# A fused attention and feed-forward step: weight loads behind the third unit's store, stack loads behind bias loads, sample copies behind splits, kept rows returned in three pieces

## The reference, cut to what matters

```
fq, fk, fv, ff, dq, dk, dv, iq, ik, iw = split(x @ w_in)         # 2892 columns, rotary on dq, dk, iq, ik
logf   = log_sigmoid(ff + b_forget)
fox    = causal attention, 8 heads x 64, logits + cumulative logf
score  = sum_h iw[h] * relu(iq[h] @ ik.T);  top 256 admissible keys per query
dsa    = attention of 8 heads (2 key heads) on these keys
h      = layer_norm(ALPHA * x + concat(fox, dsa) @ w_out)
f      = (silu(h @ w_gate) * (h @ w_up)) @ w_down                # D_FF = 2816
y      = layer_norm(ALPHA * h + f)
```

## Time and profile before

| | us |
|---|---|
| median of 3 runs | 1430.89 (1428.64 to 1433.03) |
| the profiled execution | 1433.38 |
| its span, first to last instruction | 1431.6 |
| TensorE busy | 1372.8 (96%) |
| VectorE busy | 986.7 (69%) |
| ScalarE busy | 695.2 (49%) |
| GpSimd busy | 531.6 (37%) |
| DMA moved | 192.27 MB, mean 134 GB/s |

### The profile page before, as it was taken

How to read it: one execution, slowest core, us unless ns; L and a number is a source line. 1 busy time by engine, 2 the same in 40 slices (tenths; PEclk the granted TensorE clock), 3 DMA queues, 4 the chain that set the end, 5 groups by cost and what they waited for, 6 DMA issues and landing times.

```text
span 1431.6 us, 23837 instructions
## 1 busy us (share of the span) xinstructions
PE 1372.8 (96%) x8985; PEld 1221.6 (85%) x8985; DVE 986.7 (69%) x1820; ACT 695.2 (49%) x1268; POOL 531.6 (37%) x571
## 2 busy tenths in 40 slices
PE   7989999999999899899999999999999998999997
PEld 7869989987777677687889999999999996778886
DVE  4489899778784989847775455555645656846488
ACT  5579889548684788710242223333223234524331
POOL 3632435622231022324465555555555551010011
PEclk9999999999999999999999999999999999999999
DMA  7102322358834211421124443454344449847554
GB/s 237 55 13 62 109 66 77 84 140 223 200 104 121 59 54 38 148 93 44 44 91 150 159 148 127 154 170 164 119 138 153 147 160 358 286 140 247 167 168 155
DMA packets 142738, 192.27 MB, mean 134 GB/s; under 512 B 21416, under 2 KB 99208, under 8 KB 142624
## 3 DMA queue, kind: packets, MB, share of 16 engines
q1 hardware_dynamic: 142624, 190.75, 42.2%
HBM read 134.59 MB, written 46.15 MB: 126 GB/s over the span
## 4 chain that ended last, share of the span: by engine, by line
PE 38%; POOL 8%; DVE 5%; issue 3%; ACT 1%; DMA 1%; POOLq 0%; DVEq 0%; SPq 0%; ACTq 0%
PE ffn L2676 21%; PE ffn L2191 6%; POOL w_lo L2957 5%; POOL gated L2966 3%; PE ffn L2776 3%; PE ffn L2777 3%; PE ffn L2778 3%; DVE down_lo L3041 2%; ACT w_hi L2832 1%; DMA down_raw<-in_w_down 1%; DVE rows L3175 1%; PE ffn L2650 1%; PE ffn L2795 0%; PE ffn L2793 0%; DVE ln_stats L2079 0%
## 5 line engine op out<-in xcount | busy, mean ns | idle before, releaser
L2957 POOL TENSOR_TENSOR w_lo<-w_S,w_hi 128x512 fp32r<-128x512 f32 x88 | 119.7, 1360 | 107.5 <-ACT w_hi L2832 107.5
L2676 PE MATMUL ffn<-h_T_hi,w_hi 128*128 128x264 f32 x704 | 145.6, 287 | 2.3 <-POOL w_lo L2957 2.1
L2676 PE MATMUL ffn<-h_T_lo,w_hi 128*128 128x264 f32 x704 | 143.7, 285 | 0.0
L2932 ACT CAST down_hi<-down_raw 128x1024 fp32r<-128x1024 f32 (+1 forms) x77 | 89.5, 1173 | 109.9 <-DMA down_raw<-down_w 46.5
L2676 PE MATMUL ffn<-h_T_hi,w_lo 128*128 128x264 f32 x704 | 142.8, 283 | 0.0
L2095 POOL TENSOR_TENSOR ln_rstd<-ln_var_eps,ln_power 128x1 f32<-128x1 f32 (+1 forms) x18 | 29.4, 1632 | 277.1 <-DVE ln_var_eps L2075 144.8
L3041 DVE TENSOR_TENSOR down_lo<-down_raw,down_hi 128x1024 fp32r<-128x1024 f32 (+1 forms) x77 | 105.0, 1387 | 35.0 <-ACT down_hi L2932 34.7
L2776 PE MATMUL ffn<-down_hi 128*128 128x512 f32 x308 | 121.4, 394 | 6.1 <-DVE down_lo L3041 6.1
L2832 ACT CAST w_hi<-w_S 128x512 fp32r<-128x512 f32 x88 | 54.7, 621 | 143.3 <-PE ffn L2676 141.9
L2777 PE MATMUL ffn<-down_lo,down_hi 128*128 128x512 f32 x308 | 121.0, 393 | 0.0
L2778 PE MATMUL ffn<-down_hi,down_lo 128*128 128x512 f32 x308 | 121.0, 393 | 0.0
(11 more groups left out here) (416 smaller groups left out, 3948.3 us busy)
## 6 DMA issues: line engine op xcount, KB each, us to landing
down_raw<-down_a SPq DMA_DIRECT2D x77, 256.0 KB, 3.5
gate_raw<-in_w_gate SPq DMA_DIRECT2D x11, 1024.0 KB, 6.7
up_raw<-in_w_up SPq DMA_DIRECT2D x11, 1024.0 KB, 6.4
down_t<-in_w_down SPq DMA_DIRECT2D x44, 256.0 KB, 4.1
down_w<-down_t SPq DMA_DIRECT2D x22, 512.0 KB, 3.4
down_raw<-in_w_down SPq DMA_DIRECT2D x22, 512.0 KB, 5.7
down_raw<-down_w SPq DMA_DIRECT2D x44, 256.0 KB, 4.0
down_a<-down_s SPq DMA_DIRECT2D x10, 1024.0 KB, 4.1
```

What stands on the lines that cost most here:

```text
L2676: mm = nc.tensor.matmul(pp[:, bank[to] + ch, 0:PIECE], l, x[name][:, k, ch * PIECE:(ch + 1) * PIECE], start=opens and k == 0 and i == 0, s ...
L2932: nc.scalar.copy(hs[:, 0:n], raws[s % RAWS][:, 0:n]).then_inc(hi_done, 1)
L2957: nc.gpsimd.tensor_tensor(w_lo[n % 2][:, :, :], weight(m, SCHEME[q][0]), f32(w_hi[n % 2][:, :, :]), ALU.subtract).then_inc(w_lo_done, 1)
```

## The change

- Projection: for groups 2 to 7, load_w(g + 2) goes from the beginning of group g to between the third and the fourth unit's stores.
- Attention: stack_head(6) goes from batch 6 to batch 7, behind load_bias(5); stack_head(7) from batch 7 to batch 9, behind load_bias(6).
- Start of the feed-forward: the low parts of ("S", "rest") go behind those of T3, tiles 2 and 3; the second sum then comes before them and S4 after.
- Loop: keep_samples goes from the first to the second step of an even pass, so behind one more split.
- Down projection: tiles 6 and 7 of the kept rows return in the last pass, behind load_step(0); tile 4 behind step 2, tile 5 behind step 9; the last store_s goes behind step 10. The last keep_samples, the pair copy, its low part and the last sum_activations each go behind one more step.

```diff
@@ project, sync @@
-                if g + 2 < NG:
+                if g < 2:
                     load_w(g + 2)
                 for u in OF_GROUP[g]:
                     _, t, ch = UNITS[u]
+                    if u == OF_GROUP[g][3] and 2 <= g < NG - 2:
+                        load_w(g + 2)
@@ fox, loads @@
-            if b in (2, 6):
-                stack_head(sp, b + 2 if b == 2 else 6)
-            elif b in (3, 7):
+            if b in (2, 7):
+                stack_head(sp, 4 if b == 2 else 6)
+            elif b in (3, 9):
                 stack_head(sp, 5 if b == 3 else 7)
@@ LOWERED @@
-                   ("S", "T2"), ("T2", 1), ("T2", 2), ("T2", 3)] + PAIRED[:4] + [("S", "rest")] + PAIRED[4:]
+                   ("S", "T2"), ("T2", 1), ("T2", 2), ("T2", 3)] + PAIRED[:6] + [("S", "rest")] + PAIRED[6:]
@@ mix_and_ffn, sync @@
                 if m == NM - 1:
                     load_step(0)
+                    sp.wait_ge(s_stored, s_stored_at + 16 * (NB - 1))
+                    sp.dma_start(y[:, 6:NT, :], d["kept"][2:4].rearrange("t p n -> p t n")).then_inc(rows_moved, 16)
                 if m:
                     store_t(m - 1)
...
-            for s in range(1, 5):
-                load_step(s)
+            load_step(1)
+            load_step(2)
+            sp.wait_ge(t_stored, t_stored_at + 16 * (NM - 1))
+            sp.dma_start(y[:, 4, :], d["kept"][0]).then_inc(rows_moved, 16)
+            load_step(3)
+            load_step(4)
             store_t(NM - 1)
             load_step(5)
             load_step(6)
             store_a(NB - 1)
             load_step(7)
             load_step(8)
-            sp.wait_ge(s_stored, s_stored_at + 16 * (NB - 1))
-            sp.dma_start(y[:, 6:NT, :], d["kept"][2:4].rearrange("t p n -> p t n")).then_inc(rows_moved, 16)
-            store_s(NB - 1)
             load_step(9)
             sp.wait_ge(t_stored, t_stored_at + 16 * NM)
-            sp.dma_start(y[:, 4:6, :], d["kept"][0:2].rearrange("t p n -> p t n")).then_inc(rows_moved, 16)
-            for s in range(10, STEPS):
+            sp.dma_start(y[:, 5, :], d["kept"][1]).then_inc(rows_moved, 16)
+            load_step(10)
+            store_s(NB - 1)
+            load_step(11)
+            for s in range(12, STEPS):
                 load_step(s)
@@ mix_and_ffn, tensor @@
-            pe.wait_ge(h_lo, lowered_at("T3", 3))
+            pe.wait_ge(h_lo, lowered_at("S", "rest"))
@@ mix_and_ffn, scalar @@
                     if m % 2 == 0:
-                        if q == 0:
+                        if q == 1:
                             keep_samples(m // 2 - 1)
...
-                if s == 2:
+                if s == 3:
                     keep_samples(NB - 1)
-                elif s == 3:
+                elif s == 4:
                     act.wait_ge(s_kept, NB)
@@ mix_and_ffn, vector @@
+                elif x == ("T3", 3):
+                    second_sum(0)
                 elif x == ("S", "rest"):
-                    second_sum(0)
-                elif x == ("T3", 3):
                     mix_weights(0, ("S4",))
...
-                    dve.wait_ge(rows_moved, 48)
+                    dve.wait_ge(rows_moved, 64)
...
-                if s == 3:
+                if s == 4:
                     dve.wait_ge(pair_hi, 1)
...
-                elif s == 4:
+                elif s == 5:
                     sum_activations(NB - 1)
```

## The result

| | median, us | lowest to highest | runs |
|---|---|---|---|
| before, beside it | 1429.77 | 1426.56 to 1433.03 | 6 |
| changed | 1418.63 | 1416.71 to 1423.63 | 6 |

The ratio is 0.9923, 95% interval 0.9902 to 0.9944: about 11.1 us less, where 22 were forecast. The sign was right; the time lies 9.6 us above the forecast and 0.6 us above the upper end of the range.

A forecast was written before the change was run, and what follows sets the result against it. TensorE was taken as the bound, busy 1372.8 of 1431.6 us, with pauses in five places. 5.1 + 5.4 - 0.2 + 7.0 + 4.8 = 22.1 us off 1430.89 gave 1408.8, forecast 1409, range 1403 to 1418.

The forecast's parts named there:

- A: Projection: weight loads behind the third store free ACT's stage buffers and end TensorE's pauses; gain 5.1 us, range 2 to 5.1.
- That rival (A worth 2): Projection: the key search doesn't move, so the block ends at 300.7 and the gain is 2 us; within rival 1, chance 0.20.
- 3.4 + 1.65: Projection: TensorE's two waits for an ACT copy, 3.4 us, plus 1.65 us lost at half clock behind the longer one.
- B: Attention: stack loads behind bias loads end DVE's wait for head 5's key bias; gain 5.4 us, range 2.4 to 5.9.
- Rival 1: Projection and attention: other chains take over, the search doesn't move, DVE and ACT bound the attention; 1415 us, chance 0.20.
- Rival 3: Whole kernel: each released wait is replaced by one as long; within 0.3%, about 1431 us, chance 0.04.
- C: Feed-forward start: lowering the third sample block later gives its gain back; 0.2 us loss, between gain 1.4 and loss 1.0.
- D and F: Down stage: rows returned in three pieces, sample copies behind splits; pauses before steps 3 and 10 go; 7.0 us, range 3.5 to 8.
- 0.4 us margin at step 10: Down stage: step 10's low part comes at 1212.2, TensorE needs it at 1212.6, so the pause goes with 0.4 us to spare.
- 7.0 by the row and 6.0 by the rule: Down stage gain: 7.0 us by the traced POOL product, 6.0 if the shared port lock blocks POOL's last product twice.
- E: Loop: sample copies behind splits shorten the period to 40.9 us; 0.48 us for each of ten, 4.8, range 2.1 to 4.9.
- Rival 4: Loop: ACT's copy slips, so the next block's SiLU waits for the store of the activations; 1460 us, chance 0.03.

The follow-up runs named there:

- past_only: The kernel before with only the second past group's loads moved from step 8 to step 12; median 1430.91 us, ratio 1.0005.
- only_c: The kernel before with only the rest of the sample block lowered later at the start of the feed-forward; median 1432.72 us, ratio 1.0009.
- b_past_only: The kernel before with the change's stack_head(6) and (7) moves and the second past group's loads at step 12 instead of 8; median 1429.24 us, ratio 0.9990.
- past_later_no_c: The changed kernel with the second past group's loads at step 12 and the sample block lowered where the kernel before does; median 1413.86 us, ratio 0.9884.

## Why the prediction was right and wrong

**A, forecast 5.1, by its own range 2 to 5.1: right in its mechanism.** Measured 4.9 by the medians (2.9 to 6.9) and 3.6 by the traces. The waits of ACT for output stores went (four of the ten traces keep one of 0.3 to 0.7 us), TensorE's pauses went, and the search moved along: in the changed kernel it ends at 285.7 instead of 295.95, 10 us sooner where 5.8 were reckoned. That rival (A worth 2) is out. What was mis-sized is 3.4 + 1.65: both were read in an execution that had the long pause and the half speed behind it. Over the eight traces without A they are 2.8 and 0.85 on the mean.

**B, forecast 5.4: wrong in sign, and the main cause of the miss.** Alone +4.9, undoing it -4.3: some 10 us off. The first of three steps turned the sign; the other two were mis-sized.
The first is the pacing. "Moved behind it, the six copies no longer hold SP or the DMA engines" holds for the load of head 5 alone. The prediction checked that the users of what moved (heads 6 and 7, the scales, the past keys) had over 12 us to spare, and asked of the queue only what lies ahead of head 5's key bias. The next key bias, head 6's, is loaded 16 us later on the same queue, behind stack_head(6) and the past loads and then directly ahead of stack_head(7). Before, DVE did not wait for it in the profiled trace, with 0.1 us to spare (of the other six traces without B, with the past loads in place, two show 1.52 and 0.27). After, it waits 2.39 to 6.47 us: DVE gets there sooner than the load can follow (4.0 to 4.9 us behind its issue instead of 5.5 to 6.3), and the load takes longer. "Both stay covered" was said of the copies that moved; what had to be asked is what they were moved next to.
The second is the price of a bias load with "nothing ahead", put at some 2 us. In none of the traces here did one of these 512 KB loads land in less than 3.3 us, and that of head 5 took 5.3 us in the changed kernel, when only stack_head(6)'s copies come behind it. Before it took 7.4. This error did no harm, as the load still landed 1 us before DVE wanted it.
The third is the size of the loss in the kernel before. 19.78 us against 14.35 was read in one execution. In the seven traces with B undone and the past loads in place the attention lasted 152.11, 149.07, 150.65, 149.65, 150.15, 149.90 and 148.47: the profiled execution is the longest of seven, 2.1 above their mean of 150.0. The wait for head 5's key bias was 3.25 in it; in the others it was 3.64, 1.98 (past_only), 1.80, 1.63, 0.95, 0.84 and, in only_c, none. The four traces with B and the past loads in place average 152.2. The one of B alone, 150.44, is hardly longer than the mean without B; it is the fastest of that kernel's twelve runs, and the 4.9 us are read from the medians. Rival 1 (other chains take over in B) had less gain, not a loss, and another mechanism: it named DVE's small waits on ACT. Rival 3 has the pattern, a released wait replaced by another as long, but as a thing that would have to happen in five places; none named the next load on the same queue.

**C, forecast -0.2: right, as far as can be told.** The pause was exchanged as the prediction said: the 1.49 us of the earlier trace rows for 1.9 and 0.2. A pause for POOL's low weights, 0.3 to 0.9 us, stands behind them in all seven traces with C; it had not been foreseen, but five of the eleven traces without C have it as well. By the three pairs the effect is not told from nothing; their intervals, 2 to 3 us to either side, would hide more.

**D and F, forecast 7.0, measured 6.3 alone.** The traces split it: the low parts 2 to 11 take 25.1 to 26.7 us instead of 29.3 to 30.1, some 4.1, and from there to the end it is 203.6 instead of 205.1 to 206.4, 1.5 to 2.8 for clock (b_past_only, whose clock stayed at full here without D and F, has 203.65). The pauses of 1.61 and 3.52 us in the earlier trace rows went and the 0.83 us for the rows came in their place, which the prediction missed: 5.13 less 0.83 is 4.3, and its 1.6 for the half speed makes 5.9. That the 0.4 us margin at step 10 would hold was right: no trace with D and F has a pause there.
On the port the prediction left two values, 7.0 by the row and 6.0 by the rule. POOL's products from 1090 us in the changed kernel:

```profile
L2974 POOL TENSOR_TENSOR gated<-gated,other x9: 1321/1330/2780, 1090.3 to 1177.8; 128x528 f32<-128x528 f32 x9
```

and the last two of them, beside DVE's low parts:

```profile
1172.79 2.78 POOL L2974 TENSOR_TENSOR gated<-gated,other 128x528 f32<-128x528 f32 x1 [2.31 <-DVE other L3159]
...
1177.80 2.76 POOL L2974 TENSOR_TENSOR gated<-gated,other 128x528 f32<-128x528 f32 x1 [2.23 <-DVE other L3169]
```

In the kernel before the same two products were as slow, 2.78 us at 1183.28 and 2.76 at 1188.29, so the doubling is not new. The forecast feared that the last one would be blocked twice. It was blocked once, and then DVE stood back:

```profile
1177.64 6.37 DVE L3049 TENSOR_TENSOR down_lo<-down_raw,down_hi 128x1536 fp32r<-128x1536 f32 x3
```

Three low parts of 1.75 us each would take 5.3; the second of them, step 3's, took 2.88, with POOL's product ending inside it. TensorE did not wait for what follows on ACT. The Trainium skill ("SBUF — State Buffer", section "SBUF: two separate sides"), by which the later of the two engines "fully blocks", fits both doubled products and this low part; the extra microsecond that the prediction derived from it didn't show.

**E, forecast 4.8, measured 4.65 in the traces.** The step was right in its mechanism and its size: 0.465 per block, a period of 40.9 us for 14 splits (406.15 us for 139), no pause left in the loop, and the copy still directly behind POOL's product (0.03 us, before and after). Rival 4 (the store of the activations late) didn't occur.

**The sum.** With the traces' sizes A 3.6, B -2.2, C 0, D and F 6, E 4.65 make 12.1 us; with the ratios of the parts alone 4.9 - 4.9 - 1.3 + 6.3 + 7.3 = 12.3; the changed kernel showed 11.1 and 10.0. Of the 11 us missing from the forecast of 22, B is 8 to 10, and the rest is in A's two terms and D's new pause.
The range was too narrow in one place: B's lower end was 2.4, a gain, though the edit put six copies in a place where another deadline lay. The low end should have reached to the whole of the wait it removed with the sign reversed. And the range reached up to 1418 only, from rival 1's 1415; the prediction's own sum of all low ends, 9 us, is 1422 and lies outside it.

## What to carry to other kernels

When transfers are moved behind one deadline on a queue, list the next deadline on that queue too, and everything that is issued between the two; the wait that is removed is often handed on, larger, to the next user. Ask also what the queue itself waits for: here the landing of the scales decided when the urgent load could be issued at all, so taking one wait away brought its user forward and not the load. The key bias that was late by 2.4 us in one execution was late by 6.5 in the next, so a gain read from one profiled execution should be priced by the least that other executions would show, not by that one. The same holds for a half-speed stretch behind a pause. The short periodic gain in the loop (E) is the one that a single trace told exactly.

## What the runs showed of the hardware

A 512 KB key-bias load on a busy queue varied from 6.9 to 11.3 us from issue to landing between two executions of the same kernel, at DMA shares of 1.06 and 0.99. That of head 7, with little issued ahead of it, took 3.4 to 3.9 us in 17 of 18 traces. This scatter, 4.4 us, is larger than the 3.25 us wait that the change was to remove in the attention.

The granted clock's stretches at 0.50 have no fixed place. In or behind the same 3.1 us pause at 98 us the clock fell in 14 of 18 traces and stayed at 1.00 in four. At 182 it fell in the four traces whose pause there was 2.3 to 2.9 us, and in none of the four where it was at most 1.0. The stretches at these two places were 3.4 or 6.8 us long, and half of that is lost, 1.7 to 3.4 us. The runs of one kernel differ by several microseconds along with it: past_later_no_c took 1409.48 us at a mean granted clock of 0.999 and 1417.60 at 0.994.

A low part of DVE and a product of POOL did not run side by side: the product took 2.76 us instead of 1.33, and where the next low part followed at once that one took 2.88 instead of 1.75.
